# Encoder layer on one Trainium2 core: the last four modulation steps of the MLP's norm move behind a pair of combined products and a sum of activations

## What is computed

```python
h = rms_norm(x, g_mix) * (1.0 + scale1) + shift1
z = h @ w_in
...
x = x + gate1 * mix

h = rms_norm(x, g_mlp) * (1.0 + scale2) + shift2
ff = jnp.square(jax.nn.relu(h @ w_ff1)) @ w_ff2
return x + gate2 * ff
```

## Time and profile before

| | us |
|---|---|
| three timed runs | 1406.98, 1407.10, 1407.72 (median 1407.1) |
| the profiled execution, its time | 1405.98 |
| its span, first to last instruction | 1404.2 |
| PE busy in the span | 1381.0 (98%) |
| DVE busy | 803.7 (57%) |
| ACT busy | 588.3 (42%) |
| POOL busy | 478.6 (34%) |

### The profile page before, as it was taken

How to read it: one execution, slowest core, us unless ns; L and a number is a source line. 1 busy time by engine, 2 the same in 40 slices (tenths; PEclk the granted TensorE clock), 3 DMA queues, 4 the chain that set the end, 5 groups by cost and what they waited for, 6 DMA issues and landing times.

```text
span 1404.2 us, 18642 instructions
## 1 busy us (share of the span) xinstructions
PE 1381.0 (98%) x7652; PEld 1187.7 (85%) x7652; DVE 803.7 (57%) x761; ACT 588.3 (42%) x703; POOL 478.6 (34%) x269
## 2 busy tenths in 40 slices
PE   5999999999999999999999999999999999999998
PEld 3777778898888888888888888888888888888887
DVE  5967688795438974554334543353645334344584
ACT  5667888565325632332222232332322223333152
POOL 0002111145003765574554545531432222233131
PEclk9999999999999999999999999999999999999999
DMA  9444411106210343344333343479997444445552
GB/s 369 169 158 157 155 64 38 46 31 220 111 60 31 120 162 131 138 137 151 146 117 121 120 155 142 162 290 389 374 388 269 151 150 155 165 170 198 201 191 90
DMA packets 75701, 231.30 MB, mean 165 GB/s; under 512 B 5729, under 2 KB 9953, under 8 KB 66786
## 3 DMA queue, kind: packets, MB, share of 16 engines
q1 hardware_dynamic: 75074, 229.60, 44.4%
q10 hardware_dynamic: 544, 0.52, 0.1%
HBM read 165.09 MB, written 65.01 MB: 164 GB/s over the span
## 4 chain that ended last, share of the span: by engine, by line
PE 95%; DVE 2%; DMA 1%; SPq 1%; issue 1%; ACT 0%; POOL 0%; DVEq 0%; ACTq 0%
PE bank L799 22%; PE bank L800 22%; PE bank L801 22%; PE bank L793 9%; PE bank L794 9%; PE bank L795 9%; DMA mod_first<-in_w_mod 1%; PE bank L828 1%; SPq L565 0%; PE bank L840 0%; DVE lo_r L2151 0%; DVE n_t L2123 0%; PE bank L818 0%; PE bank L810 0%; PE bank L849 0%
## 5 line engine op out<-in xcount | busy, mean ns | idle before, releaser
L799 PE MATMUL bank<-hin_hi,w_lo 128*128 128x512 f32 (+1 forms) x896 | 301.8, 337 | 0.0
L800 PE MATMUL bank<-hin_lo,w_hi 128*128 128x512 f32 (+1 forms) x896 | 301.4, 336 | 0.0
L801 PE MATMUL bank<-hin_hi,w_hi 128*128 128x512 f32 (+1 forms) x896 | 301.1, 336 | 0.0
L2528 POOL TENSOR_TENSOR w_lo<-w_raw,w_hi 128x2048 fp32r<-128x2048 f32 x28 | 134.8, 4814 | 321.8 <-ACT w_hi L1602 320.3
L2269 DVE TENSOR_TENSOR hin_lo<-hin,hin_hi 128x3072 fp32r<-128x3072 f32 x28 | 130.9, 4677 | 190.0 <-ACT hin_hi L1614 190.0
L799 PEld LDWEIGHTS bank<-hin_hi,w_lo 128*128 128x128 f32 x896 | 170.1, 190 | 18.1 <-issue 0.2
L800 PEld LDWEIGHTS bank<-hin_lo,w_hi 128*128 128x128 f32 x896 | 170.1, 190 | 17.9 <-issue 0.2
L801 PEld LDWEIGHTS bank<-hin_hi,w_hi 128*128 128x128 f32 x896 | 170.0, 190 | 17.6
L1602 ACT ACTIVATE w_hi<-w_raw 128x2048 fp32r<-128x2048 f32 x28 | 53.6, 1916 | 250.5 <-PE bank L801 188.7
L2520 POOL TENSOR_TENSOR w_lo<-w_raw,w_hi 128x512 fp32r<-128x512 f32 x43 | 65.4, 1520 | 183.9 <-ACT w_hi L1540 183.6
L1550 ACT ACTIVATE hid<-bank 128x768 f32<-128x768 f32 (+2 forms) x68 | 52.5, 773 | 162.8 <-PE bank L801 152.5
(11 more groups left out here) (293 smaller groups left out, 3169.7 us busy)
## 6 DMA issues: line engine op xcount, KB each, us to landing
hin<-hid_all SPq DMA_DIRECT2D x28, 1536.0 KB, 6.9
hid_all<-hid SPq DMA_DIRECT2D x105, 384.0 KB, 2.5
w_raw<-in_w_ff SPq DMA_DIRECT2D x36, 1024.0 KB, 9.1
mod_raw<-in_w_mod SPq DMA_DIRECT2D x16, 1024.0 KB, 6.1
w_raw<-in_w_ff SPq DMA_DIRECT2D x60, 256.0 KB, 3.4
x<-in_xT SPq DMA_DIRECT2D x5, 2048.0 KB, 14.4
w_sums<-w_raw SPq DMA_DIRECT2D x8, 1024.0 KB, 15.5
w_raw<-w_sums SPq DMA_DIRECT2D x8, 1024.0 KB, 9.7
```

The lines of the kernel that those rows point to most:

```text
L799: pe.matmul(out, w_lo, v_hi, start=first, stop=False, skip_group_check=True)
L800: pe.matmul(out, w_hi, v_lo, start=False, stop=False, skip_group_check=True)
L801: return pe.matmul(out, w_hi, v_hi, start=False, stop=last, skip_group_check=True)
L2528: pool.tensor_tensor(w2_lo[n % 2][:].rearrange("p t n -> p (t n)"), w2_raw[m % RAWS][:].rearrange("p t n -> p (t n)"), w2_hi[n % 2][:].rea ...
```

## The change

In DVE's list the second half of `norm_apply` for chunk 1 (tiles 4 to 7) goes behind U2 and C11 of job 0, the first sum of part 1 and the low part of P1's operand. In ACT's list the second half of `modulate` goes behind the high part of P1's operand of part 1 and the high part of P5's weights of job 1. Two waits are relaxed to fit: `token_hi(P1, 1)` and `token_sum(1, 1)` now wait only for tiles 0 to 3 of chunk 1 (`(2 * NN - 1) * KD + FT`, which is 44) instead of for all eight (48).

```diff
         def token_hi(i, part):
 
             v, v_hi, _ = token_operand(i, part)
-            if i in (P1, P2, P3):
+            if part and i == P1:
+                act.wait_ge(hhi_done, (2 * NN - 1) * KD + FT)
+            elif i in (P1, P2, P3):
                 act.wait_ge(hhi_done, (2 * NN if part else NN + (2 if i == P3 else 1)) * KD)
             else:
                 act.wait_ge(op_sum, 4 * part + SUM_AT[part][i])
...
         ff1_out(0, P7, S_B22, T2)
-        modulate(2 * NN - 1, range(4, KD))
         token_hi(P1, 1)
         split_w1_hi(1, P5)
+        modulate(2 * NN - 1, range(4, KD))
         token_hi(P5, 1)
...
             v = {i: token_operand(i, part)[0] for i in range(7)}
-            dve.wait_ge(hhi_done, (2 * NN - 1 + part) * KD)
+            dve.wait_ge(hhi_done, (2 * NN - 1) * KD + FT if part and step == 1 else (2 * NN - 1 + part) * KD)
             after(dve, op_sum, 4 * part + SUM_AT[part][(P5, P6, P7, P4)[step - 1]] - 1)
...
         token_lo(P4, 0)
-        norm_apply(2 * NN - 1, range(4, KD))
         hid_out(0, U2)
         hid_out(0, C11)
         token_sum(1, 1)
         token_lo(P1, 1)
+        norm_apply(2 * NN - 1, range(4, KD))
         hid_out(0, C22)
```

## The result

| | before | changed |
|---|---|---|
| timed runs, median (lowest to highest) | 1407.04 us (1405.72 to 1407.72, 6 runs) | 1411.95 us (1411.44 to 1413.14, 6 runs) |
| profiled execution | 1405.98 us | 1411.46 us |
| its span, mean granted clock | 1404.2 us, 0.998 | 1409.4 us, 0.996 |

The ratio is 1.0038, with a 95% interval of 1.0028 to 1.0048: slower by 0.38%, 4 to 6.8 us. The forecast was 1410.5.

What follows compares the result with a forecast made beforehand. PE holds 95% of the chain that ended last, so only its waits counted. Four steps 2.46 + collision 0.90 made +3.36 us at P1 of job 1: 1407.1 + 3.4 = 1410.5 us, range 1409.3 to 1413.6.

Steps and rivals of the forecast that it cites:

- The clock falls in the gap: Rival: PE's idle gap before P1 of job 1 halves its clock, adding 1.4 to 2.4 us; chance 0.17.
- DVE first: Forecast's case: DVE's moved sum gets in before POOL's sum for P5's weights; P1's low part stands 0.90 us; chance 0.38.
- POOL first: Rival: POOL's sum for P5's weights gets in before DVE's moved sum; +4.5 us in all, 1411.6; chance 0.30.
- U2 and C11 free themselves of the stall: On DVE, C11 moved ahead of the four steps ends 2.85 us earlier, removing the cause of PE's 0.54 us stall.
- Four steps behind them, +2.46: DVE's four steps end 3.66 us later without collision; PE still waits for them, so P1 of job 1 starts +2.46 us.
- The collision, +0.90 with DVE first: DVE's moved sum and low part meet two POOL sums; with DVE's sum ahead, the low part goes 0.90 us later.
- ACT nothing, late operands nothing: ACT's reordered work costs nothing; operands queued behind stay covered as PE moves 3.4 us, the tightest (P7) with 0.58 us slack.
- The clock keeps 1.00: The sum charged no clock loss for PE's gap of about 4 us before P1 of job 1.
- The wait's name: PE's list would name line 2125 (`n_t`), not C11, with 3.7 to 5 us before P1 of job 1.
- The sum: P1 of job 1's delay, 2.46 + 0.90: the last `n_t` step ends at 479.60, +3.36 us.
- Nothing is won back behind P1: PE has no slack after P1 of job 1, so what is lost there stays to the end.

Runs made afterwards that it cites:

- e3: Changed kernel, with POOL's first sum for P5's weights held until P1's low part is done and ACT's high part of them behind the modulation; 1412.05 us.
- e12: The changed kernel once more with a profile, no edit; 1411.06 us.
- e1: Changed kernel, with PE's wait for the fourth step in job 1 moved from P1 to P3; 1408.81 us, ratio 1.0017 to before.
- e2: Changed kernel, with 14 added products of 512 columns in PE's gap ahead of P1 of job 1; 1409.78 us.
- e9: Changed kernel, with 7 added products of 512 columns in PE's gap ahead of P1 of job 1; 1411.15 us.
- e4: Changed kernel, with DVE's moved sum made to wait until POOL's first sum of P5's weights is done; 1414.77 us.
- e8: Changed kernel, with PE's wait for the fourth step at P3 and the four steps ahead of the sum and P1's low part; 1407.05 us.

## Why the prediction was right, and where it was not

The path was right: PE waits at P1 for the fourth step, moved back by the order on DVE and by the collision. The time measured, 1411.95, is not that of the forecast's own sum, though, but that of its rival *The clock falls in the gap* with DVE first, and it lies in the range because the range was drawn wide enough for *POOL first* and for the cheaper half of that rival.

- **U2 and C11 free themselves of the stall**: right. C11 was forecast to end at 473.39 and ended at 473.31; with the 0.07 us by which MLP1 began earlier, that is exact.
- **Four steps behind them, +2.46**: right. Without the collision (e3) the gap grows by 2.31. The 0.15 us less is the release: I had taken the 0.37 us from C11's end to PE; from the last step to PE it was 0.20.
- **The collision, +0.90 with DVE first**: right in size and in side. The low part took 2.12 us, as forecast; e3 gives 0.87 for it. The last step was forecast at 479.60 and ended at 479.53. To me the tie was a toss; it went as the one near tie of the trace had, and DVE's sum ran whole in all five profiles in which the two start within 0.01 us (changed, e12, e1, e2, e9). *POOL first* I had priced at +4.5; e4 isn't that case, since there DVE was held until POOL's first sum had ended, so the price was not tried.
- **ACT nothing, late operands nothing**: right. P7's low part ended at 498.65, PE needed it at 500.87; PE has no new wait behind P1. e1 shows what the second one rests on: the stall itself was the cover.
- **The clock keeps 1.00**: wrong. This is the step that failed, and by the profiles the cause of most of the 1.45 us between 1410.5 and 1411.95. The sum put it at nothing. I had it as a rival at 0.17 with 1.4 to 2.4 us; in the two profiles it cost 1.57 and 1.28 behind P1, at the low end and a little under it. The rows at the program's end and start were the right ones, and I played them down because the gap was short and in the middle of the work. Neither is a reason that those rows give. The Trainium skill (TensorE: Matmul & The Clock Gate, Part 1) has half clock as the default that activity lifts; e2 and e9, where only activity was added, agree.
- **The wait's name**: wrong. I had said that the list would name line 2125; it names POOL's `w_lo` of line 2522, and "issue" in e3 and e4. The start 0.20 us behind the fourth step, and e1, show that it was the step. The list gives 3.56 us, just under the 3.7 to 5 that I had named.
- **The sum** was +3.36 and the stall's part came out at +3.18; with the clock 4.75, and 5.2 in the profile with its tail. "Nothing is won back behind P1" held.

## What to carry to other kernels

When a step moves back on an engine, look for every wait that counts it, not for the one that the profile names: P1 of job 1 uses nothing that the fourth step makes or frees, and a counter that stands at P1 and could stand at P3 cost 3.2 us. Price an idle gap of TensorE of 3 us or more with the lower clock behind it as well: here 1.28 to 1.57 us for gaps of 3 to 4 us, though one execution of e3 seems to have gone without. And a wait that goes away leaves its suppliers late: e1 won 3.7 us at P1 against the changed kernel and kept 2.5 of them until the end of MLP2.

## What was not expected of the hardware

- The clock fell after gaps of 3.08, 3.95 (twice) and 6.52 us between starts, and not where PE was idle for 1.98 us (e9) or 0.41 (e2). It fell inside the gap (e3, e4, e12) or one microsecond behind it (the first profile). It took 1.28 to 2.45 us.
- It also fell without a gap, at 296 to 298 us in e2, e3 and e8 and about 2 us earlier in e9, in products of 128 columns without a pause (PE busy 2.00 of 2.00 in every window); in the same stretch of the kernel before it read 1.00.
- With starts at most 0.01 us apart, POOL's record the earlier in two of five profiles (473.23 against 473.24 in the changed kernel), DVE's sum ran whole each time; with POOL 0.07 us ahead (e4, 474.64 against 474.71) POOL's did.
- How often the clock falls after a gap of 3 us, why it falls without one, and what sets whether it falls inside the gap or behind it, stays open.
